# A fourth weight slot in a hand-ordered two-block kernel

## What is computed

```
h = layer_norm(a*x + stick_breaking_attention(x @ sb_win) @ mix_wo)        # stages sb, wo
h = layer_norm(a*h + cross_attention(h @ xa_wq, mem @ xa_wkv) @ xa_wo)     # mem, xq, xo
h = layer_norm(a*h + (gelu(g) * val) @ ffn_down)                           # up, down
      # g, val = halves of short_conv(h @ ffn_up)
p = rms_norm(h) @ w_in                                                     # rwkv, conv, pool, gates
ys = rwkv7(p_rwkv), short_conv(p_conv), pooling(p_pool)
out = sum(sigmoid(p_gate[n]) * (ys[n] @ w_branch[n])) @ w_out              # branch, out
x = h + rms_norm(out)
```

## Time and profile before

| | us |
|---|---|
| median of 3 runs | 1496.7 (1496.17 to 1496.83) |
| the profiled execution's own time | 1498.02 |
| its span in the profile | 1496.3 |
| TensorE busy | 1435.3 (96%) |
| GpSimd, ScalarE, VectorE busy | 749.4, 640.9, 588.0 |
| the 16 DMA engines busy with the weight queue | 24.0% of the span |

### The profile page before, as it was taken

The page is one execution under the profiler, slowest core; times in us unless marked ns, Lnnn a source line. Parts: engine busy times, 40 slices in busy tenths (PEclk is TensorE's granted clock), DMA queues, the critical chain, the costliest instruction groups (busy, mean ns, idle before and its releaser), DMA issues.

```text
span 1496.3 us, 22841 instructions
## 1 busy us (share of the span) xinstructions
PE 1435.3 (96%) x8776; PEld 1160.5 (78%) x8776; DVE 588.0 (39%) x697; ACT 640.9 (43%) x1038; POOL 749.4 (50%) x595
## 2 busy tenths in 40 slices
PE   7999999999998999999999799899999999999997
PEld 5877777677776888888888477688878888888876
DVE  5455554553255333333223426332327433221123
ACT  4555555445335444444322556343335333222343
POOL 3443434255345655555545346753326665444564
PEclk9999999999999999999999999999999999999998
DMA  5222222221122232222333122200012322222222
GB/s 185 85 77 79 85 71 77 78 95 60 57 71 70 99 99 91 93 97 99 105 107 105 50 85 72 69 17 3 3 32 95 120 93 96 91 96 98 98 96 87
DMA packets 35505, 122.88 MB, mean 82 GB/s; under 512 B 3936, under 2 KB 6240, under 8 KB 35296
## 3 DMA queue, kind: packets, MB, share of 16 engines
q1 hardware_dynamic: 34848, 119.64, 24.0%
q10 hardware_dynamic: 576, 2.06, 0.4%
HBM read 119.59 MB, written 2.10 MB: 81 GB/s over the span
## 4 chain that ended last, share of the span: by engine, by line
PE 65%; issue 19%; POOL 9%; DVE 3%; ACT 2%; POOLq 0%; DMA 0%; ACTq 0%; DVEq 0%; SPq 0%
PE ps L454 14%; PE ps L455 14%; PE ps L456 14%; POOL w_lo L1658 8%; PE ps L1051 2%; PE ps L1052 2%; PE ps L1053 2%; PE ps L1022 2%; PE ps L1129 1%; PE ps L1128 1%; PE ps L1127 1%; PE ps L1008 1%; PE ps L846 1%; PE ps L483 1%; PE ps L484 1%
## 5 line engine op out<-in xcount | busy, mean ns | idle before, releaser
L1658 POOL TENSOR_TENSOR w_lo<-stage,w_hi 128x512 fp32r<-128x512 f32 x434 | 589.9, 1381 | 641.9 <-ACT w_hi L1155 641.7
L1155 ACT ACTIVATE w_hi<-stage 128x512 fp32r<-128x512 f32 x434 | 249.6, 623 | 440.6 <-DMA stage<-w 429.5
L454 PE MATMUL ps<-x_hi,w_lo 128*128 128x512 f32 x936 | 370.4, 396 | 4.8 <-POOL w_lo L1658 4.8
L456 PE MATMUL ps<-x_hi,w_hi 128*128 128x512 f32 x936 | 365.4, 390 | 0.0
L455 PE MATMUL ps<-x_lo,w_hi 128*128 128x512 f32 x936 | 365.2, 390 | 0.0
L454 PEld LDWEIGHTS ps<-x_hi,w_lo 128*128 128x128 f32 x936 | 176.2, 188 | 44.7 <-DVE rw_vz L2033 5.9
L455 PEld LDWEIGHTS ps<-x_lo,w_hi 128*128 128x128 f32 x936 | 176.3, 188 | 37.2 <-issue 1.7
L456 PEld LDWEIGHTS ps<-x_hi,w_hi 128*128 128x128 f32 x936 | 176.1, 188 | 37.0
L1998 DVE SCALAR_TENSOR_TENSOR conv<-ps,vcol,conv 128x511 f32<-128x511 f32 x44 | 33.0, 750 | 147.8 <-ACT conv L1321 147.8
L2220 DVE TENSOR_TENSOR bt<-gates,ps 128x512 f32<-128x512 f32 x24 | 16.3, 679 | 140.3 <-PE ps L1129 140.3
L454 PE MATMUL ps<-f_hi,w_lo 128*128 128x512 f32 x176 | 68.5, 389 | 0.0
(11 more groups left out here) (361 smaller groups left out, 2539.1 us busy)
## 6 DMA issues: line engine op xcount, KB each, us to landing
stage<-w SPq DMA_DIRECT2D x217, 512.0 KB, 3.6
outT<-H SPq DMA_DIRECT2D x16, 128.0 KB, 1.7
H<-xT SPq DMA_DIRECT2D x3, 512.0 KB, 7.7
mem<-memT SPq DMA_DIRECT2D x2, 512.0 KB, 10.1
pool_n<-pool_count ACTq DMA_DIRECT2D x1, 1024.0 KB, 5.9
H<-xT SPq DMA_DIRECT2D x2, 256.0 KB, 4.7
w_small<-small ACTq DMA_DIRECT2D x1, 512.0 KB, 4.1
con<-const SPq DMA_DIRECT2D x1, 448.0 KB, 8.9
```

The source lines that it names most:

```text
L454: pe.matmul(out, wl, hi(k), start=first, stop=False)
L456: mm = pe.matmul(out, wh, hi(k), start=False, stop=end)
L1155: act.activation(w_hi[:, b % RING, cols], stage[:, b % RING, cols], ACT.Copy).then_inc(whi_made, 1)
L1658: pool.tensor_tensor(w_lo[:, b % RING, cols], stage[:, b % RING, cols], w_hi[:, b % RING, cols].bitcast(F32), ALU.subtract).then_inc(wlo_m ...
```

## The change

The ring gets four slots. Unit u's transfer waits for unit u-4 instead of u-3, and unit 3's transfer goes out with the first ones, behind all other loads of the start. The distance at which ScalarE and GpSimd split is a constant of its own, AHEAD = 3, so both engines do the same instructions in the same order as before. The 8 KB per partition for the slot (4 KB of `stage`/`w_lo` and 4 KB of `w_hi`) come from the space reserved for dynamic DMAs, cut from 16384 to 1024 bytes; every other tile lies 8064 bytes lower. Since three units a tile do not divide by four slots, the down projection's loops are written out. A few semaphores of VectorE's are merged into one (`link_s`), each still set and awaited at the same instruction.

```diff
+SCRATCH = 1024
-RING = 3
+RING = 4
+AHEAD = 3
-UP_TURN = UP_BANKS * RING
+UP_TURN = UP_BANKS * AHEAD
...
-        BASE = 17408
-
-        w_lo = at("w_lo", [P, RING, UNIT], 0, F32R)
-        stage = at("stage", [P, RING, UNIT], 0)
-        w_hi = at("w_hi", [P, RING, UNIT], 12, F32R)
+        BASE = SCRATCH + 128 + 2 * RING * 1024
+
+        w_lo = at("w_lo", [P, RING, UNIT], -2 * RING, F32R)
+        stage = at("stage", [P, RING, UNIT], -2 * RING)
+        w_hi = at("w_hi", [P, RING, UNIT], 2 * RING, F32R)
...
+            sp.dma_start(stage[:, 3, :], w[3]).then_inc(landed[3], 16)
             with sp.Fori(1, UNITS // RING) as i:
                 for j in range(RING):
...
-            with pe.Fori(1, KB // 2 - 1) as i:
-                for j in range(2):
-                    pe.wait_ge(y_made, 2 * i + (j + BEFORE["y_made"]["down"] + CREDIT - 1))
-                    down_tile(2 * i + j, 2 * DOWN_UNITS * i + (U0["down"] + DOWN_UNITS * j), j)
-            for t in range(KB - 2, KB):
+            for t in range(2, KB):
                 pe.wait_ge(y_made, t + (BEFORE["y_made"]["down"] + CREDIT - 1))
                 down_tile(t, U0["down"] + DOWN_UNITS * t, t % 2)
...
                     if k < KB - 1:
-                        split_hi(U0[n] + k + RING)
+                        split_hi(U0[n] + k + AHEAD)
...
-            with act.Fori(0, KB // 2 - 1) as i:
-                for k in range(1, 3):
-                    down_splits(k, i)
+            for k in range(1, KB - 1):
+                down_splits(k)
```

More of the change, by code:

```diff
@@ L768, in down_tile @@
                 for c in range(DOWN_UNITS):
-                    product(ps[:, bank, :], u + c, (U0["down"] + c) % RING,
+                    product(ps[:, bank, :], u + c, (u + c) % RING,
                             lambda k: f_hi[:, 8 * c + k, :], lambda k: f_lo[:, 8 * c + k, :],
@@ L1147, in _, with split_hi @@
             act.sem_inc(evac, CREDIT)
-            def split_hi(b, i=0, turns=0):
-                act.wait_ge(landed[b % RING], 16 * turns * i + 16 * (b // RING + 1))
+            def split_hi(b, i=0, step=0):
+                act.wait_ge(landed[b % RING], 16 * (step // RING) * i + 16 * (b // RING + 1))
                 for part in range(2):
@@ L1355, in _, with down_splits @@
             act.preload_act_table_set("natural_log_exp_and_others")
-            def down_splits(k, i=0, last=False):
+            def down_splits(k, last=False):
                 for c in range(DOWN_UNITS):
                     if c == DOWN_UNITS - 1:
-                        square_of("down", 2 * i + k, k % 2)
+                        square_of("down", k, k % 2)
                     if c < DOWN_UNITS - 1 or not last:
-                        split_hi(U0["down"] + DOWN_UNITS * k + c + RING, i, 2)
+                        split_hi(U0["down"] + DOWN_UNITS * k + c + AHEAD)
             down_splits(0)
-            with act.Fori(0, KB // 2 - 1) as i:
-                for k in range(1, 3):
-                    down_splits(k, i)
+            for k in range(1, KB - 1):
+                down_splits(k)
             down_splits(KB - 1, last=True)
@@ L1400, in _ @@
             scaled(1)
-            split_hi(U0["rwkv"] + RING)
+            split_hi(U0["rwkv"] + AHEAD)
             for t in range(2, 5):
@@ L1632, in _ @@
                 act.activation(sqv[:, j % 2, :], Y[:, j, :], ACT.Square).then_inc(sq_made, 1)
-                if b + RING < UNITS:
-                    split_hi(b + RING)
+                if b + AHEAD < UNITS:
+                    split_hi(b + AHEAD)
             last = U0["out"] + KB - 1
@@ L1666, in splits @@
                     split_lo(u)
-            splits(0, UNITS_OF["sb"] + RING)
+            splits(0, UNITS_OF["sb"] + AHEAD)
             def split_x(n):
@@ L1675, in split_x @@
                                        ALU.subtract).then_inc(x_ready, 1)
-            splits(U0["wo"] + RING, KB)
+            splits(U0["wo"] + AHEAD, KB)
             split_x("wo")
-            splits(U0["mem"] + RING, KB + 1)
-            splits(U0["xo"] + RING, KB)
+            splits(U0["mem"] + AHEAD, KB + 1)
+            splits(U0["xo"] + AHEAD, KB)
             split_x("xo")
@@ L1701, in _ @@
             ff_low(FFB - 1, (2 * FFB - 2) % UP_BANKS)
-            splits(U0["down"] + RING, DOWN_UNITS * KB)
+            splits(U0["down"] + AHEAD, DOWN_UNITS * KB)
             with pool.Fori(0, KB) as k:
@@ L1706, in _ @@
                                    ALU.subtract).then_inc(x_ready, 1)
-            for t in range(RING, 12):
+            for t in range(AHEAD, 12):
                 split_lo(U0["rwkv"] + t)
@@ L1825, in _ @@
             split_lo(U0["out"] + 2)
-            for j in range(KB - RING):
-                split_lo(U0["out"] + j + RING)
+            for j in range(KB - AHEAD):
+                split_lo(U0["out"] + j + AHEAD)
             for half in range(2):
@@ L1837, in _, with link @@
             dve.sem_inc(mv_taken, CREDIT)
+            chain = [0]
+            def link(ins):
+                chain[0] += 1
+                ins.then_inc(link_s, 1)
+                dve.wait_ge(link_s, chain[0])
             for a, (k0, k1) in enumerate(X_PIECES):
@@ L2009, in _ @@
             norm("down")
[L2010 to L2016, removed]
             dve.memset(tiny[:], TINY).then_inc(rw_cols_s, 1)
```

60 lines of the change are left out of this document (25 added, 35 removed).

## The result

The changed kernel takes 1493.05 us (median of 12 runs, 1491.25 to 1494.06), the kernel before 1496.43 in the same comparison (12 runs, 1495.41 to 1498.9). The ratio is 0.9977, with a 95% interval of 0.9969 to 0.9985: 3.4 us, 0.23%, just over the 0.2% that the prediction took as the least that can be told from no change. (Such a ratio need not be the quotient of the two medians beside it.) The forecast was 1494.4. The profiled execution has a span of 1491.3 us where that of before has 1496.3; more than the medians differ by, since the profiled execution of before (1498.02) is one of its slower ones.

The account below looks back on a forecast made before the run. TensorE, busy 96% of the span, was taken as the bound. Three waits of 2.42 us less about 0.1 for the port gave 2.3 us off the 1496.7 us median: 1494.4 us, range 1491.5 to 1497.8.

Parts of the forecast that it names:

- the long wait goes: Rival, 6%: TensorE's 4.84 us wait at `rwkv` unit 13 goes too, if ScalarE's transfer wait delays VectorE's chain; 1489.4 us.
- the port falls out well: Rival, 16%: earlier GpSimd splits spare VectorE shared-port hold-ups before line 569 in some head pairs; 2 to 4 us more gained.
- Three waits go whole, 2.42 us: TensorE's waits for late transfers in `wo`, `xo` and `out` vanish with four slots: 0.53 + 0.47 + 1.42 us.
- about 0.1 for the port: Deduction in the sum for VectorE and GpSimd sharing an SBUF port: 2.42 us less about 0.1 gives 2.3.
- 3.6 us lost against 2.3 won: Range's slow end: one instruction fetch for the unrolled down projection costs 3.6 us against the 2.3 us gain; 1497.8 us.
- Unit 13's wait stays: TensorE's 4.84 us wait in `rwkv` comes from GpSimd's order of work, with no transfer in the chain; term 0.
- The port, 0: Before 924.91 us, GpSimd's earlier unit 8 split shifts a VectorE hold-up to `L2047`; 0, bounds 1.0 gained, 1.3 lost.
- Line 569's 7.4 us don't move: Waits at line 569, ending VectorE's chain beside GpSimd's splits in eight head pairs, should stay at 7.4 us.
- port rival: Two rivals on line 569's head pairs: hold-ups spared, 1490.5 to 1492.5 us (16%), or added in seven pairs, 1501.3 (8%).
- Unrolling the down projection, at nothing: Writing out the down projection's loops neither costs nor gives anything; at worst one instruction fetch of 3.6 us.
- Addresses, scratch, unit 3's transfer, 0: Lower tile addresses, smaller dynamic DMA scratch and unit 3's transfer at the start were each priced at nothing.
- The base of the sum: Start of the sum: profiled execution of the kernel before, 1498.02 us, taken as 1.3 us above the runs' median 1496.7.

Follow-up runs that it names:

- the last experiment: Changed kernel with ScalarE's split of `rwkv` unit 13 sooner and GpSimd's splits of units 12 and 13 before its third multiplication: 1488.04 us, 0.9931 of the kernel before.

## Why the prediction was right, and where it was not

The number was right to 1.4 us and its sign was right; a good part of what it added up came about by something else. The three waits and the long one were read rightly, but that the number fell so near is in part luck. The likeliest verdict, no change (66%), did not come: 1493.05 is under the 1493.7 of "faster by over 0.2%", given 27%, and neither of the two ways that were priced there (the long wait goes, the port falls out well) is how it came about.

- **Three waits go whole, 2.42 us.** They did, and TensorE's waits for `w_lo` fell from 7.0 to 5.0 us. But 1.1 us of that comes with the shorter landing, in a ring of three and at its pace: the wait in `wo` (0.53) is gone there without an earlier transfer. The earlier transfer takes the other 0.9. By the matmuls' starts the term is sized rightly for transfers of 3.6 us; they were no longer that. The sum takes "about 0.1 for the port" off it, where the working has 0 for the port; and the upper end of the range, 3.6 us lost against 2.3 won, would be 1498.0 and not 1497.8.
- **Unit 13's wait stays.** 4.84 to 4.78 us. The reading of the earlier trace rows was right, and the last experiment shows it from the other side: moving GpSimd's order takes it away.
- **The port, 0, with `L2047` near 3.3 us and `L2050` short.** Right: from `L2045` to `L2052` it is 5.64 us before and 5.65 after. The same instructions of VectorE after:

```profile
893.27 3.33 DVE L2039 TENSOR_TENSOR rw_L<-rw_L,cen 128x2048 f32<-128x2048 f32 x1
896.52 1.25 DVE L2041 TENSOR_TENSOR gfac<-cen 128x12 f32<-128x12 f32 x1
897.81 0.17 DVE L2042 COPY gfac<-cen 128x4 f32<-128x4 f32 x1
```

  2.29 became 3.33, 1.22 became 0.17, and what follows lost nothing. By the rule of the Trainium skill (SBUF — State Buffer, "Who interferes with whom"), that the one who issues first holds the port for its whole instruction, the trace agrees: GpSimd's half that began at 893.16, just ahead of this row at 893.27, took its usual 1.29 us, and the half behind it, at 894.42, took 3.33. Elsewhere more moved than the term allows for, likely by the same port: in the down projection VectorE's 26 instructions took 17.47 us for 30.53 (the window after and the earlier trace rows), as its two-input additions took 0.69 us each for 1.77 and 1.52, and over the span VectorE was busy for 572.9 us in place of 588.0. That too goes with the shorter landing (574.1 in the kernel that was only unrolled), and behind the start no wait of TensorE for VectorE got shorter by it.
- **Line 569's 7.4 us don't move.** 7.4 us, so neither port rival came about there.
- **Unrolling the down projection, at nothing.** This is the step that failed, as the prediction put it: "neither form costs or gives anything". In its place, where it stands, that is so. But a longer TensorE program made transfers land about 0.4 us sooner (3.6 to 3.2 or 3.3, medians), which the prediction's sum has no term for. TensorE unrolled alone is worth 0.13% (0.04 to 0.22), unrolled with ScalarE 0.21% (0.11 to 0.30), where the waits account for 1.1 to 1.4 us. In the profiles most of the rest lies in how long the clock was low behind two waits, as told above; why is open. The start has no clear part in it: TensorE's first matmul came at 8.30 to 8.56 us in the nine profiles of short landing and at 8.49 to 9.10 in the five of long, and the kernel with ScalarE unrolled, of long landing, has the earliest 31st matmul of all (17.1 us, against 17.4 to 20.6).
- **Addresses, scratch, unit 3's transfer, 0.** 0.9994 and no difference that can be told: right.
- **The base of the sum.** The profiled execution of before was slow at its start: its second group of matmuls waited another 0.90 us. In 14 profiles this wait is there in two, both of the kernel before; the three others with the same TensorE program don't have it, and their ratios are 0.9994 to 1.0002, so it is more likely chance; it is not shown. Nor is the low clock only where the text ahead of the prediction puts it, in the first slice: the page's clock row has 9 in every slice but the last, and windows over single waits, as 845 to 865 us (0.91) or 940 to 960 (0.83), show it low behind them.

What stays open: what in the chip makes the packets at a transfer's start slower under one length of TensorE's program than under others. One more packet of the instruction queue goes with it, and so would a place in memory that shifts with the program's length; a program that was longer still did not bring the slow transfers back, and no run here moved the weights by themselves. The Trainium skill (DMA: Bandwidth & Descriptors, "Latency and other measured facts") tells of copies that run slower when their rows lie a large power of two apart in HBM. No run here shows that this is the case, and the 4 KB between the rows of a unit are the same in all kernels.

## What to carry to other kernels

Idle time of an engine that feeds the bound one is no measure of what a deeper ring gives: the earlier transfer took 323 us of it away here (382.5 to 59.7) for 0.9 us of TensorE's. Follow each wait of the bound engine back to what came last; if that is the order of another engine's work, as it was at the longest wait, slots do nothing until they are used to change the order, and that was worth more (some 5 us) than the whole change. And where a change comes in parts, run the ones that look like bookkeeping alone: the part costed at nothing, in a kernel of its own, took off 0.21% (0.11 to 0.30) where the whole change took 0.23% (0.15 to 0.31).

## What the runs showed that I had not expected

- The time from a transfer's issue to its landing, 512 KB each, went with the length of TensorE's program, which neither issues nor moves it: 3.6 to 3.7 us with 6624 TensorE instructions in the built program, 3.2 to 3.3 with 6720 to 6948, in 13 kernels and 14 profiles, whatever the loops, the tiles' addresses, the ring or GpSimd's program (228 instructions longer). Only one length has the long landing, so where it begins and ends is not known.
- 228 empty instructions behind TensorE's last product took longer than the time that is left there, less than 11 us from that product to the end of the span: the span ended 8.2 us behind the last send of an output and not 2.1.
- Where a long wait of TensorE goes, the low clock behind it goes too. After its 4.78 us the matmuls from 941.12 on started 0.43 us apart up to 944.96 (the level of 1.2 GHz), and 0.23 after (2.4 GHz); with a wait of 0.26 us at this place they started 0.23 us apart throughout, 2.0 us less over ten matmuls. Of the lead that both together give, 1.1 us is lost again by 956 us (951 in the faster kernel). How long the low clock lasts behind one and the same wait is not fixed: twelve or thirteen matmuls in four profiles and six in ten, behind the wait at 850 us, 1.2 to 1.4 us apart in time.
